# Attention scores from split operands, with the residual kept in DRAM and attention-stage weights in one buffer

## Chip, cores and metric

One NeuronCore of a Trainium2 chip runs the whole program. The time is the device time of one execution in microseconds (us); a comparison takes the median over executions.

## What is computed

The reference is a block with differential attention, a gated convolution and a gated feed-forward part, followed by two retention layers, all in float32, on 512 tokens of width 1024. The change touches the first block's attention:

```python
h = jnp.concatenate([meta, x], axis=1)           # 16 + 512 tokens
n = _rms(h, norm_mix_w[l])
z = n @ w_in[l]
q, k, v, glu, g_att, g_conv = jnp.split(z, splits, axis=-1)
...
s = jnp.einsum('bqhmd,bkhmd->bhmqk', qb, kf)     # 8 heads, two halves m of 64 each
mask = cid[None, :] <= qc[:, None]
p = jax.nn.softmax(jnp.where(mask, s, NEG_INF), axis=-1)
a = p[:, :, 0] - lam * p[:, :, 1]
return jnp.einsum('bhqk,bkhe->bqhe', a, vf)
...
h = h + m @ w_out[l]
```

## The kernel before

Activations lie transposed, features in partitions and tokens in columns. H (`o_h`) is the residual, K, Q and V_ the keys, queries and values of the 8 heads in float32, each head's two halves in rows 0 to 63 and 64 to 127. The large matrix products are made of three rounded (float32r) products: high weight by high input, high by low, low by high. For this, each weight slot of 128x1024 is split: ScalarE copies it into the rounded format (`high`, L1386), VectorE subtracts that from the raw weights (`low`, L2337). Raw weights come as units of 1 MB (256 columns by 8 k tiles, two slots each) from SyncE's queue (L3563) into three raw buffers of 8 KB per partition, unit u into buffer u % 3; a buffer is refilled once the last slot in it has been split. Units 28 to 31 are `w_conv_out`, 32 to 35 `w_out`, from 36 (`first_ffn`) on the feed-forward weights come through two buffers, and `S1T` and two more weight tiles lie where the third was.

All engines run fixed programs in order; semaphores (T, V, A, G for TensorE, VectorE, ScalarE, GpSimd) tie them, and an engine that waits holds back everything behind. The order around the change is written out by hand:

- 16 gate tiles (L870), each 48 products on TensorE, with the layer norm of the convolution beside them on VectorE and ScalarE: squares after gates 8 and 9, five diagonals (L2592) and a scaling after gate 12, for which TensorE waits when gate 12 is done.
- 32 attention steps i = 4h + r, head h, r = 0 to 3, whose query tile t comes from ORDER = (1, 2, 0, 3); t has 144 + 128 t key columns (t = 3: 16 and 512). TensorE does `scores(i)` (L888, plain float32), `turn(i-2)` (transposes of the probabilities, L899, L901), `values(i-3)` (L911, L913) and filler products of `conv_out_quarter` (L659: none at r=0, one quarter at r=1 and 2, two at r=3). VectorE does `combine(i-1)` (L2627 to L2635) and `highest(i)` (mask L2617, negated maximum L2621; the order of the two differs by r), then the convolution gating (L2664), at r=0 a weight split and the sum of a head (L2655), at r=1 the head's low part (`head_split`, L2659). ScalarE does `turn(i-2)` (L1622, L1625), `values(i-3)` (L1632, L1634) and `soften(i)` (exponentials with sums, L1614), at r=2 scalings of a finished head (L1640), at r=3 a weight split.
- Scores of t=0, 1, 2 use banks 0 and 1 or 2 and 3 in turn; t=3 needs all four, so it waits for the exponentials of both steps ahead of it.
- Then `w_out` (units 32 to 35) and `ffn_token` (L2776), which adds its result to H.

## Time and profile before

| | us |
|---|---|
| median of 3 runs | 1810.76 (1806.86 to 1813.85) |
| the profiled execution | 1809.18, span 1807.4 |
| TensorE busy | 1788.2 |
| VectorE busy | 1406.6 |
| ScalarE busy | 968.6 |
| mean granted TensorE clock | 0.999 of 2.4 GHz |

The page gives, for the slowest core, each engine's busy time, the span in slices, the chain of work that ended last and the costliest groups of instructions. The attention stage runs from about 354 to 484 us of the span, the gate stage before it from about 259.

### The profile page before, as it was taken

To read this page: it belongs to the slowest core of one execution; us is meant where nothing else is said; L and a number is where in the kernel's file an instruction comes from. 1 tells how busy PE (TensorE), PEld (TensorE's weight loads), DVE (VectorE), ACT (ScalarE), POOL (GpSimd) and SP (SyncE) were. 2 spreads that over 40 slices of the span, in tenths; PEclk is the share of its full clock that TensorE was granted. 3 is DMA by queue.
4 is the path that set the end of the run, shared out by engine and by line. 5 is a ranking of instruction groups with operands and counts; after the bars stand their busy time and mean duration, and the time that the engine had idled before them with its cause. 6 is when DMAs were issued, how large, how long until landed. Compare 5 with 4: busy or idle time off the path is not lost.

```text
span 1807.4 us, 32723 instructions
## 1 busy us (share of the span) xinstructions
PE 1788.2 (99%) x13606; PEld 1706.0 (94%) x13606; DVE 1406.6 (78%) x2464; ACT 968.6 (54%) x1894; POOL 164.5 (9%) x138
## 2 busy tenths in 40 slices
PE   9999999999999999999999999999999999999998
PEld 8999999978899989899899999999899999999987
DVE  5888897678756789869889797979358888888844
ACT  6223332568734447547566565657347566666632
POOL 0000000000000012011011212120000112121000
PEclk9999999999999999999999999999999999999999
DMA  5222222200132257566357777775333677777431
GB/s 198 94 81 84 94 94 71 94 24 25 63 108 74 79 136 169 128 158 146 107 125 156 158 157 153 158 154 126 117 94 81 131 163 149 160 150 162 116 118 70
DMA packets 251778, 213.47 MB, mean 118 GB/s; under 512 B 6646, under 2 KB 248111, under 8 KB 251630
## 3 DMA queue, kind: packets, MB, share of 16 engines
q1 hardware_dynamic: 185086, 178.34, 32.0%
q0 software_dynamic: 66528, 33.04, 14.9%
q8 instruction: 107, 1.75, 0.4%
q14 instruction: 41, 0.34, 0.1%
q10 hardware_dynamic: 16, 0.00, 0.0%
HBM read 209.26 MB, written 2.10 MB: 117 GB/s over the span
## 4 chain that ended last, share of the span: by engine, by line
PE 90%; DVE 5%; ACT 3%; DMA 1%; issue 0%; SPq 0%; DVEq 0%
PE ps L659 41%; PE ps L700 31%; PE ps L1300 5%; PE ps L1352 5%; DVE wlo L2337 1%; PE ps L888 1%; DMA raw<-in_w_up_dram 1%; PE ps L1141 1%; PE ps L1119 1%; PE ps L913 1%; PE ps L1132 1%; PE ps L1144 1%; ACT p L1614 1%; ACT whi L1386 0%; DVE ast L2621 0%
## 5 line engine op out<-in xcount | busy, mean ns | idle before, releaser
L2337 DVE TENSOR_TENSOR wlo<-raw,whi 128x1024 fp32r<-128x1024 f32 (+1 forms) x363 | 440.0, 1216 | 193.7 <-ACT whi L1386 192.3
L1386 ACT ACTIVATE whi<-raw 128x1024 fp32r<-128x1024 f32 (+1 forms) x363 | 380.6, 1050 | 245.3 <-PE ps L659 105.5
L659 PE MATMUL ps<-nhi,whi 128*128 128x256 f32 (+3 forms) x1392 | 316.8, 291 | 2.6 <-DVE clo L2605 0.8
L659 PE MATMUL ps<-nhi,wlo 128*128 128x256 f32 (+3 forms) x1392 | 312.5, 288 | 0.0
L659 PE MATMUL ps<-nlo,whi 128*128 128x256 f32 (+2 forms) x1264 | 275.4, 288 | 0.0
L659 PEld LDWEIGHTS ps<-nhi,whi 128*128 128x128 f32 x1392 | 227.3, 190 | 6.6 <-DVE clo L2605 1.0
L659 PEld LDWEIGHTS ps<-nhi,wlo 128*128 128x128 f32 x1392 | 226.4, 189 | 2.1
L700 PE MATMUL ps<-thi,whi 128*128 128x256 f32 x784 | 225.3, 287 | 1.2 <-DVE wlo L2337 0.5
L700 PE MATMUL ps<-thi,wlo 128*128 128x256 f32 x784 | 222.1, 283 | 0.0
L700 PE MATMUL ps<-tlo,whi 128*128 128x256 f32 x784 | 221.9, 283 | 0.0
L700 PE MATMUL ps<-nhi,whi 128*128 128x256 f32 (+1 forms) x756 | 216.1, 286 | 0.0
L700 PE MATMUL ps<-nhi,wlo 128*128 128x256 f32 (+1 forms) x756 | 213.3, 282 | 0.0
L700 PE MATMUL ps<-nlo,whi 128*128 128x256 f32 (+1 forms) x756 | 213.1, 282 | 0.0
L659 PEld LDWEIGHTS ps<-nlo,whi 128*128 128x128 f32 x1264 | 201.9, 189 | 1.9
L2507 DVE SCALAR_TENSOR_TENSOR c<-u,cv,c 128x514 f32<-128x514 f32 x240 | 163.2, 750 | 0.0
L700 PEld LDWEIGHTS ps<-thi,whi 128*128 128x128 f32 x784 | 150.0, 191 | 3.4 <-ACT kr L1410 1.4
L700 PEld LDWEIGHTS ps<-tlo,whi 128*128 128x128 f32 x784 | 150.0, 191 | 0.0
L700 PEld LDWEIGHTS ps<-thi,wlo 128*128 128x128 f32 x784 | 149.8, 191 | 0.0
L700 PEld LDWEIGHTS ps<-nhi,wlo 128*128 128x128 f32 x756 | 143.5, 190 | 0.0
L700 PEld LDWEIGHTS ps<-nlo,whi 128*128 128x128 f32 x756 | 143.3, 190 | 0.1
L700 PEld LDWEIGHTS ps<-nhi,whi 128*128 128x128 f32 x756 | 143.3, 189 | 0.1
L3504 POOL DMA_DIRECT2D raw<-in_w_in_dram x49 | 62.9, 1284 | 514.1 <-DMA raw<-in_w_in_dram 514.1
(473 smaller groups left out, 3655.8 us busy)
## 6 DMA issues: line engine op xcount, KB each, us to landing
raw<-in_w_in_dram SPq DMA_DIRECT2D x90, 1024.0 KB, 5.8
raw<-in_w_up_dram SPq DMA_DIRECT2D x22, 1024.0 KB, 5.2
raw<-in_w_out_dram SPq DMA_DIRECT2D x20, 1024.0 KB, 4.8
s1t<-in_w_in_dram SPq DMA_DIRECT2D x49, 256.0 KB, 3.1
s1t<-in_w_in_dram POOLq DMA_DIRECT2D x49, 256.0 KB, 7.1
raw<-in_w_in_dram POOLq DMA_DIRECT2D x49, 256.0 KB, 4.7
raw<-in_w_down_dram SPq DMA_DIRECT2D x16, 512.0 KB, 3.4
raw<-in_w_conv_out_dram SPq DMA_DIRECT2D x4, 1024.0 KB, 4.8
```

The source lines that it names most:

```text
L659: mm = eng.matmul(o, w, m[:, k, a:b], start=begins, stop=final and n == len(ks) - 1 and i == 2)
L700: mm = eng.matmul(o, w[:, k, :], m[:, k, :], start=start and k + i == 0, stop=stop and k == 3 and i == 2, skip_group_check=True)
L888: eng.matmul(sv[:, m, c0 + a:c0 + b], Q[r, h, 2 + 128 * t:130 + 128 * t], K[r, h, a:b], start=True, stop=True) \
L913: mm = eng.matmul(o, at_[:, j, :], V_[:, 1 + j, vc], start=False, stop=j == t)
L1119: mm = eng.matmul(P[:, z1 + 128 * n:z1 + 128 * n + 128], KR[c][:, x], QR[c][:, x], start=True, stop=True)
L1132: mm = eng.matmul(P[:, z + 128 * n:z + 128 * n + 128], KTK[:, n, :], VTK[:, n, 128 * c:128 * c + 128], start=True, stop=True)
L1300: mm = eng.matmul(P[:, 512 * b:512 * b + 256], x_[:, k, 128 * t:128 * t + 128], w_[:, k % 4, :], start=k + i == 0, stop=k == 7 and i == 2)
L1352: mm = eng.matmul(P[:, 512 * b:512 * b + 512], x_[:, k, 128 * t:128 * t + 128], w_[:, 0, w], start=k == 0 and i == 0, stop=k == 15 and i == 2)
L1386: eng.activation(hi, raw, ACT.Copy).then_inc(*A.up("hi", s))
L2337: eng.tensor_tensor(lo, raw, hi.bitcast(F), ALU.subtract).then_inc(*V.up("lo", s))
L2507: eng.scalar_tensor_tensor(C[:, f, :], src, c, C[:, f, :], ALU.mult, ALU.add).then_inc(*V.up("tap", f, tap))
L3504: eng.dma_start(quarters_of(v)[1], plan[v][0][:, 0:4, 0:128], accum_op=ALU.add).then_inc(*THIRD_IN[s1_of(v)].up("unit", v))
```

## The change

Four things together.

1. Keys and queries are split like weights: KHI, QHI are rounded copies by ScalarE (`key_high`, `query_high`), KLO, QLO the rest by VectorE (`key_low`, `query_low`), written over K and Q. A score is the sum of three rounded products (high by high, low query by high key, high query by low key) in one bank, for both halves.
2. KHI lies where H was. So H is written to a DRAM tensor `kept` early (at slot 8 of SyncE's queue, after the tokens are turned), and read back in four quarters after the last scores; each pair of `ffn_token` waits for its quarter.
3. QHI takes raw buffers 1 and 2. Units 29 to 32 therefore come one after the other through buffer 0; unit 33 (buffer 1) is loaded only after the last scores, and from there on two buffers alternate.
4. Keys are split at gates 10 to 13, the meta tokens and query 0 at gate 13, queries 1 and 2 at gate 14, and queries 3 to 7 at r=1 of heads 0 to 4.

```diff
--- before.py
+++ after.py
@@ -204,6 +204,10 @@
         V_ = at("v", [128, 5, D], F, o_v)
         Q = at("q", [128, NH, TQ], F, o_q)
         GA = at("ga", [128, NH, TQ], F, o_ga)
+
+        KHI, KLO = at("khi", [128, NH, T1], R, o_h), at("klo", [128, NH, T1], R, o_k)
+        QHI, QLO = at("qhi", [128, NH, T2], R, o_raw + 8192), at("qlo", [128, NH, TQ], R, o_q)
+        kept = nc.dram_tensor("kept", [128, KT, T1], F).ap()
 
         XT = at("xt", [128, 4, D], F, o_k)
         XM = at("xm", [128, D], F, o_k + 16384)
@@ -375,7 +379,9 @@
         assert len(place) == len(slots)
         before = [max((r for r in range(s) if place[r] == place[s]), default=None) for s in range(len(slots))]
         pairs_from = next(u for u in range(first_ffn, first_ffn + 3) if u % 3 == 0)
-        rawbuf = [u % 3 if u < pairs_from else (u - pairs_from) % 2 for u in range(len(plan))]
+        attention_from = first_ffn - 8
+        rawbuf = [u % 3 if u <= attention_from else 0 if u < first_ffn - 3 else (u - first_ffn) % 2 for u in range(len(plan))]
+        after_scores = first_ffn - 3
         follows = [next((v for v in range(u + 1, len(plan)) if rawbuf[v] == rawbuf[u]), None) for u in range(len(plan))]
         sevens = [u for u in range(len(plan)) if plan[u][1] is SEVEN]
 
@@ -592,11 +598,17 @@
         ROWS_IN, FM_IN, FR_IN, LAM_IN, CST_IN, POS_IN, FAR_IN, PBC_IN = [
             Signal(sem(f"{n}_in"), 16) for n in ("rows", "norm", "ffn_rows", "lambda", "const", "positions", "decay", "post")]
         EARLY_IN = [Signal(sem(f"early_in{i}"), 16) for i in range(2)]
+        H_OUT, H_IN = Signal(sem("h_out"), 16), [Signal(sem(f"h_in{i}"), 16) for i in range(4)]
         RAW_IN = [Signal(sem(f"raw_in{i}"), 16) for i in range(3)]
         QUARTER_IN, SUM_IN, THIRD_IN = [[Signal(sem(f"{n}_in{i}"), 16) for i in range(2)] for n in ("quarter", "sum", "third")]
         OUT_SENT = [Signal(sem(f"out_sent{i}"), 16) for i in range(5)]
-        signals = [T, V, A, G, *X_IN, ROWS_IN, FM_IN, FR_IN, LAM_IN, CST_IN, POS_IN, FAR_IN, PBC_IN, *EARLY_IN, *RAW_IN,
+        signals = [T, V, A, G, *X_IN, ROWS_IN, FM_IN, FR_IN, LAM_IN, CST_IN, POS_IN, FAR_IN, PBC_IN, *EARLY_IN, H_OUT, *H_IN, *RAW_IN,
                    *QUARTER_IN, *SUM_IN, *THIRD_IN, *OUT_SENT]
+
+        KEYS_AT = {10: (0, 1), 11: (2, 3, 4), 12: (5,), 13: (6, 7)}
+
+        def last_slot_of(u):
+            return max(s for s, slot in enumerate(slots) if slot[0] == u)
 
         def raw_in(u, k0=0):
             if u < 2 and k0 == 0:
@@ -881,12 +893,16 @@
             def scores(i):
                 h, t, nk = head(i)
                 sv, c0, banks = where(i)
+                qh, ql = QHI[:, (h + 4) % NH, 128 * t:128 * t + 128], QLO[:, h, 2 + 128 * t:130 + 128 * t]
                 for a, b in [(0, nk)] if t < 3 else [(0, NM), (NM, nk)]:
-                    for m in range(2):
-                        r = slice(64 * m, 64 * m + 64)
-                        on.wait_ge(A("q", h), A("k", h), *free(*banks[m]))
-                        eng.matmul(sv[:, m, c0 + a:c0 + b], Q[r, h, 2 + 128 * t:130 + 128 * t], K[r, h, a:b], start=True, stop=True) \
-                            .then_inc(*T.up("scores", i, m, a))
+                    kh, kl = KHI[:, h, a:b], KLO[:, h, a:b]
+                    for n, (q_, k_) in enumerate(((qh, kh), (ql, kh), (qh, kl))):
+                        for m in range(2):
+                            r = slice(64 * m, 64 * m + 64)
+                            on.wait_ge(A("qh", h), V("ql", h), A("kh", h), V("kl", h), A("kh_meta"), V("kl_meta"), *free(*banks[m]))
+                            mm = eng.matmul(sv[:, m, c0 + a:c0 + b], q_[r], k_[r], start=n == 0, stop=n == 2)
+                            if n == 2:
+                                mm.then_inc(*T.up("scores", i, m, a))
                 for m in range(2):
                     emptied(banks[m], A("exp", i, m))
 
@@ -1567,6 +1583,18 @@
                 on.wait_ge(V("centre", f), f > 1 and V("squares", f - 2))
                 eng.activation(SQ[f % 2], C[:, f, :], ACT.Square).then_inc(*A.up("ln_square", f))
 
+            def key_high(h):
+                on.wait_ge(A("k", h), H_OUT("sent"))
+                eng.activation(KHI[:, h, NM:T1], K[:, h, NM:T1], ACT.Copy).then_inc(*A.up("kh", h))
+
+            def key_high_meta():
+                on.wait_ge(A("k", 7), T("mini_scores"))
+                eng.activation(KHI[:, :, 0:NM], K[:, :, 0:NM], ACT.Copy).then_inc(*A.up("kh_meta"))
+
+            def query_high(h):
+                on.wait_ge(A("q", h), V("lo", last_slot_of(attention_from if h > 3 else attention_from - 2)))
+                eng.activation(QHI[:, (h + 4) % NH, :], Q[:, h, 2:TQ], ACT.Copy).then_inc(*A.up("qh", h))
+
             for i, (kind, f) in enumerate(GATES):
                 w.take()
                 w.done()
@@ -1593,6 +1621,12 @@
                 elif i == 13:
                     on.wait_ge(T("mini_scores"))
                     eng.activation(STS, P[0:NM, MB:MB + 32], ACT.Copy).then_inc(*A.up("mini_scores"))
+                    key_high_meta()
+                    query_high(0)
+                for h in KEYS_AT.get(i, ()):
+                    key_high(h)
+                for h in (1, 2) if i == 14 else ():
+                    query_high(h)
 
 
             def ln_split(fs):
@@ -1690,6 +1724,8 @@
                     head_scale(h - 2)
                 if r == 0 and h >= 3:
                     head_sum(h - 3)
+                if r == 1 and h < 5:
+                    query_high(h + 3)
 
 
             turn(30)
@@ -2570,6 +2606,18 @@
                 eng.tensor_scalar(nx[0:2, 4:5], P[0:2, 3076:3077], 1.0 / D, LN_EPS, ALU.mult, ALU.add).then_inc(*V.up("var_rest"))
                 rsqrt(("ln_rms",), rcol[:, 0:5], nx[:, 0:5], na[:, 0:5], V("var_rest"))
 
+            def key_low(h):
+                on.wait_ge(A("kh", h))
+                eng.tensor_tensor(KLO[:, h, NM:T1], K[:, h, NM:T1], KHI[:, h, NM:T1].bitcast(F), ALU.subtract).then_inc(*V.up("kl", h))
+
+            def key_low_meta():
+                on.wait_ge(A("kh_meta"))
+                eng.tensor_tensor(KLO[:, :, 0:NM], K[:, :, 0:NM], KHI[:, :, 0:NM].bitcast(F), ALU.subtract).then_inc(*V.up("kl_meta"))
+
+            def query_low(h):
+                on.wait_ge(A("qh", h))
+                eng.tensor_tensor(QLO[:, h, 2:TQ], Q[:, h, 2:TQ], QHI[:, (h + 4) % NH, :].bitcast(F), ALU.subtract).then_inc(*V.up("ql", h))
+
             for i in range(16):
                 w.take()
                 if i == 11:
@@ -2595,6 +2643,13 @@
                         on.wait_ge(A("ln_spread"), V("centre", f))
                         eng.scalar_tensor_tensor(C[:, f, :], C[:, f, :], cv[:, f, CLNW:CLNW + 1], LNR, ALU.mult, ALU.mult) \
                             .then_inc(*V.up("ln_scaled", f))
+                elif i == 13:
+                    key_low_meta()
+                    query_low(0)
+                for h in KEYS_AT.get(i, ()):
+                    key_low(h)
+                for h in (1, 2) if i == 14 else ():
+                    query_low(h)
 
 
             def ln_split(fs):
@@ -2735,6 +2790,8 @@
                     head_sum(h - 3)
                 if r == 1 and h >= 3:
                     head_split(h - 3)
+                if r == 1 and h < 5:
+                    query_low(h + 3)
 
 
             combine(31)
@@ -2772,7 +2829,7 @@
 
             def ffn_token(f):
                 j, c = f // 2, f % 2
-                on.wait_ge(*([T("out", 0, c, n) for n in range(2)] if j == 0 else [T("out", j, c)]))
+                on.wait_ge(H_IN[j]("in"), *([T("out", 0, c, n) for n in range(2)] if j == 0 else [T("out", j, c)]))
                 eng.tensor_tensor(H[:, f, Q0:T1], H[:, f, Q0:T1], tile_dst(PAIR["out", j, c], TQ)[0], ALU.add).then_inc(*V.up("out", f))
                 on.wait_ge(A("nh", f, False))
                 eng.scalar_tensor_tensor(NLO[:, f, 0:TQ], H[:, f, Q0:T1], cv[:, f, WFFN:WFFN + 1], NHI[:, f, 0:TQ].bitcast(F),
@@ -3493,7 +3550,7 @@
                     eng.dma_start(S1T[n % 2], plan[u][0][:, 4:8, 128:256], accum_op=ALU.add).then_inc(*SUM_IN[n % 2].up("unit", u))
 
             for s, (u, box, final) in enumerate(slots):
-                if rawbuf[u] == 2 and final and follows[u] is None:
+                if u == first_ffn - 1 and final:
                     first_sum(0)
                     first_sum(1)
                 if box_of(s)[1] == 1:
@@ -3538,7 +3595,7 @@
                     u = sevens[n]
                     if n > 1:
                         on.wait_ge(V("second_sum", sevens[n - 2]), V("lo", slot_of[sevens[n - 2], 1]))
-                    on.wait_ge(V("lo", raw2_read))
+                    on.wait_ge(V("lo", raw2_read), T("scored", 7))
                     eng.dma_start(S1T[n % 2], plan[u][0][:, 0:4, 128:256]).then_inc(*QUARTER_IN[n % 2].up("unit", u))
 
             raw2_read = max(s for s, (u, _, _) in enumerate(slots) if rawbuf[u] == 2)
@@ -3552,15 +3609,23 @@
                 elif s == len(slots) - 14:
                     on.wait_ge(T("mixed_all"))
                     eng.dma_start(PBC, post_norm_2[1:2, :].to_broadcast([128, D])).then_inc(*PBC_IN.up("in"))
-                if rawbuf[u] == 2 and final and follows[u] is None:
+                if u == first_ffn - 1 and final:
                     first_sum(0)
                     first_sum(1)
                 if box_of(s)[1] == 1:
                     first_sum(sevens.index(u) + 2)
+                if s == 8:
+                    on.wait_ge(A("h", 6, 1))
+                    eng.dma_start(kept, H).then_inc(*H_OUT.up("sent"))
                 v = follows[u]
-                if final and v:
+                if final and v and v != after_scores:
                     on.wait_ge(V("lo", s))
                     eng.dma_start(raw_of(v), plan[v][0]).then_inc(*RAW_IN[rawbuf[v]].up("unit", v))
+                if final and v == after_scores - 1:
+                    on.wait_ge(T("scored", 7), H_OUT("sent"))
+                    eng.dma_start(raw_of(after_scores), plan[after_scores][0]).then_inc(*RAW_IN[rawbuf[after_scores]].up("unit", after_scores))
+                    for j in range(4):
+                        eng.dma_start(H[:, 2 * j:2 * j + 2, :], kept[:, 2 * j:2 * j + 2, :]).then_inc(*H_IN[j].up("in"))
             for t in range(4):
                 for n, (f0, f1) in enumerate([(0, 8)] if t < 3 else [(0, 4), (4, 8)]):
                     on.wait_ge(V("out_ready", t, n))
```

ScalarE at r=1 and r=2 of head 2, before (i=9 and 10; `p` is the probabilities, `at` their transpose, `ps` PSUM):

```order
L1614 ACTIVATE p_1_114,ast<-ps,ast 128x400 [waits vector_done]
L1614 ACTIVATE p_1_117,ast<-ps,ast 128x400
L1622 ACTIVATE at_118<-ps 128x256 [waits tensor_done]
L1625 ACTIVATE at_118<-ps 16x128
L1614 ACTIVATE p_2_115,ast<-ps,ast 128x144 [waits vector_done]
L1614 ACTIVATE p_0_116,ast<-ps,ast 128x144
L1632 ACTIVATE os_123<-ps,ast 128x128 [waits tensor_done]
L1634 ACTIVATE ps,ss<-ps,ast 128x128 [waits scalar_done]
```

and in the change:

```order
L1648 ACTIVATE p_0_117,ast<-ps,ast 128x400 [waits vector_done]
L1648 ACTIVATE p_1_121,ast<-ps,ast 128x400
L1596 ACTIVATE qhi<-q 128x512
L1656 ACTIVATE at_122<-ps 128x256 [waits tensor_done]
L1659 ACTIVATE at_122<-ps 16x128
L1648 ACTIVATE p_1_118,ast<-ps,ast 128x144 [waits vector_done]
L1648 ACTIVATE p_0_120,ast<-ps,ast 128x144
L1666 ACTIVATE rbc<-ps,ast 128x128 [waits tensor_done]
L1668 ACTIVATE ps,ss<-ps,ast 128x128 [waits scalar_done]
```

The copy of a query stands behind both exponentials of t=2 (400 columns) and ahead of the transposes and the exponentials of t=0 (144 columns).

VectorE over the same steps, before, from the combination of t=1:

```order
L2635 SCALAR_TENSOR_TENSOR p_2_115<-p_0_116,ast,p_2_115 128x272 [waits vector_done]
L2617 MEMSET ps 64x2x64 [waits tensor_done]
L2372 SCALAR_TENSOR_TENSOR rcol<-na,rcol 128x4 [waits vector_done]
L2621 TENSOR_REDUCE ast<-ps 128x2 [waits vector_done]
L2617 MEMSET ps 64x2x64 [waits tensor_done]
L2364 SCALAR_TENSOR_TENSOR na<-rcol 128x4 [waits vector_done]
L2621 TENSOR_REDUCE ast<-ps 128x2 [waits vector_done]
```

and in the change:

```order
L2690 SCALAR_TENSOR_TENSOR p_2_119<-p_0_120,ast,p_2_119 128x272 [waits vector_done]
L2672 MEMSET ps 64x2x64 [waits tensor_done]
L2408 SCALAR_TENSOR_TENSOR rcol<-na,rcol 128x4 [waits vector_done]
L2676 TENSOR_REDUCE ast<-ps 128x2 [waits vector_done]
L2619 TENSOR_TENSOR qlo<-q,qhi 128x512 [waits scalar_done]
L2672 MEMSET ps 64x2x64 [waits tensor_done]
L2400 SCALAR_TENSOR_TENSOR na<-rcol 128x4 [waits vector_done]
L2676 TENSOR_REDUCE ast<-ps 128x2 [waits vector_done]
```

The subtraction, which waits for ScalarE's copy, stands between the maximum of t=2 (the first TENSOR_REDUCE) and the mask and maximum of t=0 (the second).

SyncE's queue from the second unit of `w_conv_out` to the last of `w_out`, before (raw_49, 50 and 51 are the raw buffers 0, 1 and 2):

```order
L3563 DMA raw_51<-in_w_conv_out_dram 128x8x256 [waits vector_done]
L3563 DMA raw_49<-in_w_conv_out_dram 128x8x256 [waits vector_done]
L3563 DMA raw_50<-in_w_conv_out_dram 128x8x256 [waits vector_done]
L3563 DMA raw_51<-in_w_out_dram 128x8x256 [waits vector_done]
L3563 DMA raw_49<-in_w_out_dram 128x8x256 [waits vector_done]
L3563 DMA raw_50<-in_w_out_dram 128x8x256 [waits vector_done]
L3563 DMA raw_51<-in_w_out_dram 128x8x256 [waits vector_done]
```

and in the change:

```order
L3623 DMA raw_49<-in_w_conv_out_dram 128x8x256 [waits vector_done] x3
L3623 DMA raw_49<-in_w_out_dram 128x8x256 [waits vector_done]
L3626 DMA raw_50<-in_w_out_dram 128x8x256 [waits h_out,tensor_done]
L3628 DMA h<-kept 128x1056 x4
L3623 DMA raw_49<-in_w_out_dram 128x8x256 [waits vector_done]
L3623 DMA raw_50<-in_w_out_dram 128x8x256 [waits vector_done]
L3623 DMA raw_49<-in_w_up_dram 128x8x256 [waits vector_done]
```

Three units in a row share buffer 0, and the second unit of w_out waits for TensorE, with the four reads of H behind it.

## Rows read from the trace of the kernel before

**Rows 1.** The page, busy time and share of TensorE (PE).
```profile
PE 1788.2 (99%) x13606; PEld 1706.0 (94%) x13606; DVE 1406.6 (78%) x2464; ACT 968.6 (54%) x1894; POOL 164.5 (9%) x138
```

**Rows 2.** Busy per stretch: us, PE, PEld, DVE, ACT, POOL, clock, DMA, GB/s.
```profile
366.92:384.70 17.78, 16.78 (x118) 13.57 (x118) 10.31 (x31) 10.65 (x38) 0.00 (x0) 0.90 0.00 1
...
413.31:427.96 14.65, 14.60 (x115) 12.13 (x115) 11.95 (x39) 12.19 (x43) 0.00 (x0) 1.00 0.22 73
```

**Rows 3.** The chain in order of time, attention: start, us, what.
```profile
398.73 1.28 PE ps L888 x8
...
424.53 0.98 DVE ast L2621
425.53 1.26 ACT p L1614 x4
...
427.19 0.72 ACT p L1614 x4
427.96 1.35 PE ps L888 x8
```

**Rows 4.** Timeline of TensorE, one head: start, us, line, operation.
```profile
433.72 0.73 PE L888 MATMUL ps<-k,q 64*128 64x272 f32 x4
434.38 0.28 PE L899 MATMUL ps<-ident,p 128*16 128x128 f32 x1
...
439.00 0.52 PE L888 MATMUL ps<-k,q 64*128 64x144 f32 x4
439.51 0.27 PE L899 MATMUL ps<-ident,p 128*16 128x128 f32 x1
```

**Rows 5.** Timeline: first records of 272 columns, loads; then means by form.
```profile
433.72 0.50 PE L888 MATMUL ps<-k,q 64*128 64x272 f32 x2
...
427.96 0.53 PEld L888 LDWEIGHTS ps<-k,q 64*128 64x128 f32 x8 [0.26 <-ACT p L1614]
...
L888 PE MATMUL ps<-k,q 64*128 64x400 f32 x24 | 5.7, 548 | 0.0
L888 PE MATMUL ps<-k,q 64*128 64x272 f32 x24 | 4.4, 442 | 0.0
```

**Rows 6.** The chain over the span: rounded products, 264 and 512 columns.
```profile
41.86 129.22 PE ps L659 x1056
...
1718.39 82.65 PE ps L1352 x363
```

**Rows 7.** Timeline: copies on ScalarE, subtractions on VectorE.
```profile
354.53 3.75 ACT L1602 ACTIVATE nhi<-c 128x514 fp32r<-128x514 f32 x7
...
357.95 2.50 DVE L2605 TENSOR_TENSOR clo<-c,nhi 128x514 fp32r<-128x514 f32 x4
```

**Rows 8.** Timeline of VectorE: mask and maximum of t=0.
```profile
440.76 0.17 DVE L2617 MEMSET ps<- 64x128 f32 x1
...
440.96 0.46 DVE L2621 TENSOR_REDUCE ast<-ps 128x2 f32<-128x288 f32 x1
```

**Rows 9.** Timeline of ScalarE: first exponential of t=2, heads 0 to 3.
```profile
364.07 0.59 ACT L1614 ACTIVATE p<-ps,ast 128x400 f32<-128x400 f32 x1 [1.71 <-DVE ast L2621]
...
380.42 0.59 ACT L1614 ACTIVATE p<-ps,ast 128x400 f32<-128x400 f32 x1
...
395.97 0.59 ACT L1614 ACTIVATE p<-ps,ast 128x400 f32<-128x400 f32 x1 [0.88 <-DVE ast L2621]
...
410.88 0.59 ACT L1614 ACTIVATE p<-ps,ast 128x400 f32<-128x400 f32 x1
```

**Rows 10.** Timeline: diagonals on VectorE, gate 12 on ScalarE.
```profile
331.51 0.99 DVE L2592 TENSOR_SCALAR sq<-ident,rcol 128x128 f32<-128x128 f32 x5
...
334.59 0.60 ACT L1580 ACTIVATE ga<-ps 128x514 f32<-128x514 f32 x1 [4.26 <-PE ps L659]
```

**Rows 11.** DMA issues of the page; then ScalarE's first split of unit 33.
```profile
raw<-in_w_conv_out_dram SPq DMA_DIRECT2D x4, 1024.0 KB, 4.8
...
485.10 1.04 ACT L1386 ACTIVATE whi<-raw 128x1024 fp32r<-128x1024 f32 x1
```

## Prediction

> **What bounds the kernel now.** I read the page first: TensorE is busy for 99% of the span [rows 1], so a thing costs time if it lengthens TensorE's own work or makes TensorE wait. The change lives in the attention stage, so next I cut the stretch view at the start of each head's last score step (query tile 3, "t=3"; within a head the order is t=1, 2, 0, 3). A settled head takes 14.65 us, with TensorE almost full but VectorE and ScalarE at 11.9 and 12.2 us [rows 2]: all three are near their limit, so the chain of waits must tell who leads. It does [rows 3]: up to 425.5 it runs on VectorE, which comes late to the 0.98 us maximum of t=2, then on ScalarE (exponentials of t=2, 1.26; of t=0, 0.72), and only then does TensorE start t=3 at 427.96. Head 2's t=3 at 398.73 follows in the same chain straight on TensorE's own products. So in heads 1 and 2 TensorE leads; from head 3 on, the loop is t=3's scores and the products after it, VectorE up to the maximum of t=2, ScalarE up to the exponential of t=0.
>
> **Scores on TensorE.** A float32 score product of 272 columns is two passes over two weight loads; the two halves of the head (rows 0 to 63, 64 to 127) run side by side. From its start to the next operation: 434.38 - 433.72 = 0.66 us for 272 columns, 0.51 for 144 (439.51 - 439.00) [rows 4]. The first two records last 0.50, the mean of all is 442 ns, so the second two last 0.39: the first pays about 0.11 us for a weight load in the open, the second's load is hidden behind the first's columns [rows 4, 5]. Loads of one pair after another come 0.113 us apart ((0.53 - 0.19) / 3) [rows 5]. Rounded (float32r) products take one pass: 129.22 / 1056 = 0.122 us for 264 columns, 82.65 / 363 = 0.228 for 512 [rows 6], 0.42 ns a column, against 0.83 x 2 for float32 ((548 - 442) / 128 per half). So four passes become three. A group costs 0.11 (first load) + 3 x the larger of 0.113 and the columns + 0.1 (the gap behind): 272 columns 0.11 + 0.35 + 0.1 = 0.56, saved 0.10; 400 columns 0.11 + 0.51 + 0.1 = 0.72 against 0.88 by the same law, saved 0.16; 144 columns 0.11 + 0.34 + 0.1 = 0.55 against 0.51, nothing saved, since loads set the pace; t=3 (16 + 512 columns) 0.45 + 0.64 + 0.1 = 1.2 against 1.28 (its 1.35 in [rows 3] less the 0.07 by which 0.73 exceeds 0.66), saved 0.1. No row has a rounded product under 256 columns or on 64 rows. Bounds: columns of the 144 form at the float32 price (0.24 a product) give 0.93, that is +0.4 a head; the two halves one after the other give rival B.
> Here a rule of the Trainium skill speaks against the change. The records say that a second load into the same rows was hidden [rows 4, 5]. The page TensorE: Matmul & The Clock Gate, section Part 3: Packing small matmuls, says that "LDWEIGHTS overlaps with in-flight MATMULs only when row_grp differs". By that rule each product would show its load; the trace of this kernel contradicts it, so I keep it as rival C.
> Where TensorE leads (heads 1, 2) 0.35 us a head is saved; in head 3 some 0.25; from head 4 only t=3's 0.1, since VectorE sets when t=2's maximum starts. Sum: -0.7 - 0.25 - 0.4 = **-1.35 us**.
>
> **The new splits inside the attention loop.** Heads 0 to 4 get `query_high` on ScalarE and `query_low` on VectorE at step r=1, for the head three further on. A copy of 514 columns takes ScalarE 0.62 (seven in 3.75: 0.52 apart), a subtraction takes VectorE 0.69 (four in 2.50: 0.60 apart) [rows 7]. The lengths matter less than the place. `query_low` waits for `query_high`, which is queued behind both exponentials of t=2; and behind `query_low`, on VectorE, wait the mask and maximum of t=0 (0.20 + 0.46 [rows 8]), which today run while ScalarE works on t=2. Behind these wait the exponential of t=0, and TensorE's t=3, whose banks it frees. From the start of t=2's exponential: 1.15 (both) + 0.62 + 0.05 + 0.60 + 0.20 + 0.46 + 0.1 + 0.72 + 0.05 = 3.95 us. I compare with today's distances [rows 2, 3, 9] (the starts of t=3 are the bounds of the stretches): head 4, 427.96 - 425.53 = 2.43, so +1.5; head 3, 413.31 - 410.88 = 2.43, +1.5; head 2, 398.73 - 395.97 = 2.76, +1.2; head 1, 384.70 - 380.42 = 4.28, nothing; head 0, 366.92 - 364.07 = 2.85 with a small copy of the 16-token part in it (0.2), +1.3. Sum **+5.5 us**. Bounds: below, 0.53 a head if VectorE came by chance to the subtraction with nothing due (+1.5 in all); above, the same 3.95 with head 1 uncovered, +6.5. I take 5.5, since the order on both engines is fixed.
>
> **Splits in the gate stage.** Eight keys, three queries and the meta tokens: about 11 x 0.53 = 5.8 us on ScalarE and 11 x 0.60 = 6.6 on VectorE between gates 10 and 14. They lie beside 30 us of TensorE work. The tightest place is gate 11: three keys put the weight split and the five diagonals back from 331.51 by some 1.6 us, so they would end at 331.51 + 0.99 + 1.6 = 334.1, and TensorE asks for them when gate 12 ends, about 334.5 [rows 10]. Cost 0; if that cover is short by some tenths, +0.3.
>
> **Transfers.** Keeping H is one write of 2.16 MB at slot 8 and four reads after the last scores. A 1 MB unit lands in 4.8 us [rows 11]; by size the write takes some 10 us in a stage in which a buffer is refilled two units ahead. With one buffer, the next convolution unit starts after the split of the last one and is wanted three steps later, some 10 us; it needs 4.8. Unit 33 now starts only after t=3 of head 7 (about 473) and lands near 478; its first split runs at 485.10 [rows 11], 7 us spare. H arrives in quarters until about 486; the additions that want it follow TensorE's first w_out tiles, whose last weights are split after 485.10. Cost 0; what would be late next is unit 33, and each us past 485 would be one us of TensorE.
>
> **Sum.** The profiled execution took 1809.2 us (span 1807.4); -1.35 + 5.5 = +4.1, so **1813 us**. That execution lies 1.6 under the median of the runs, well inside their spread. A measurement of this kernel tells about 0.5%, 9 us, from no change; this is within it.
>
> **Rivals.**
> A, the forecast: a new wait of ScalarE and VectorE eats more than the passes give. 1813. Chance 0.60.
> B, the one that ends slower: rounded products on 64 rows do not run side by side. For: no row shows such a pair. Against: float32 halves start together. A group then has six products in a row: t=3 2.2 instead of 1.28, t=2 1.27, t=1 0.92, t=0 0.86. It decides as soon as the pair's second half waits for the first; heads 1 and 2 lose 1.6 each, heads 3 to 7 about 1.1 to 1.25: +9 in place of -1.35, 1809.2 + 5.5 + 9 = 1824. Chance 0.09.
> C, each product shows its weight load (the rule above), or a narrow operand is no quicker: 0.21 more a group, twice in t=3, is +4; the narrow form alone is +0.4 in four heads, 1.6. 1815 to 1817. Chance 0.10.
> D, the clock. In head 0's long period the granted clock is 0.90 of 17.78 us, which is 1.8 / 0.5 = 3.5 us at 1.2 instead of 2.4 GHz; TensorE was busy in it for 16.78 only [rows 2]. That cost some 1.7 us. Four heads now get a wait of 1.2 to 1.5 us. If each brings such a fall, +1.7 to +6.8: 1815 to 1820. Against: the stretch up to head 4's t=3 holds 1.00 though it too ends in a wait [rows 2, 3]. The Trainium skill, same page, section A second HAM failure mode: psum-queue depth-cycling, says that short idle times between groups of matmuls make the clock swing between its levels; by that rule this case is the likely one, and in the trace only one of the eight heads bears it out. Chance 0.12.
> E, the new chain is mostly covered and only the passes count: 1808 to 1810. For: ScalarE and VectorE each have over 2 us free a head. Chance 0.07.
> F, the change does more than it says, over 9 us gained: even all passes saved without any wait give 8 x 0.35 = 2.8. Chance 0.02.
>
> **Numbers.** Slower by over 0.5% means beyond 1818: B whole, the upper half of D, and 0.02 for a late unit or H: 0.17. Faster 0.02. Within 0.5%: 0.81. The range takes A with its bounds (1809 to 1815), C, E and most of D: 1806 to 1820.
>
> **What would show it.** Right: score groups of 0.56 and 0.72 us with both halves starting together; on VectorE, in heads 2 to 4, a wait of the subtraction for the query's copy of about 0.6 to 1 us and TensorE idle 1.2 to 1.5 us before t=3; heads 5 to 7 at about 14.5 us; no wait for unit 33 or H. Wrong: halves one after another, more than one stretch at 1.2 GHz, a wait of the first w_out split for its load, or heads 2 to 4 still at 14.6.

## The result, and the profile after

The changed kernel takes 1816.84 us (median of 4 runs, 1815.78 to 1819.14) against 1808.81 for the kernel before on the same chip (4 runs, 1806.56 to 1813.85): a ratio of 1.0051, 95% interval 1.0035 to 1.0066. On a second chip it took 1818.98 (4 runs) against 1806.48 (14 runs), 1.0061, 1.0040 to 1.0082. The forecast was 1813, with a range of 1806 to 1820. So the time lies in the range and about 4 us above the forecast. Both intervals lie clear of 1: the change makes the kernel slower, by half a per cent. In the forecast's own terms the ratio stands just beyond the 0.5% inside which it put the result with a chance of 0.81, though the intervals reach to both sides of that mark. The profiled execution took 1817.56, with a span of 1815.8, 8.4 more than before.

TensorE's share on the page after, for [rows 1]. It is busy for 1.6 us more, in a span that is 8.4 us longer:

```profile
PE 1789.8 (99%) x13686; PEld 1713.8 (94%) x13686; DVE 1416.4 (78%) x2481; ACT 978.6 (54%) x1911; POOL 164.6 (9%) x138
```

Busy time per stretch after, as [rows 2], each from one start of t=3 to the next (us, PE, PEld, DVE, ACT, POOL, clock, DMA share, GB/s). The first ends with t=3 of head 1, the last with that of head 6:

```profile
368.41:386.07 17.66, 16.53 (x126) 14.23 (x126) 10.02 (x26) 10.80 (x37) 0.00 (x0) 0.90 0.00 1
386.07:402.52 16.45, 14.16 (x121) 12.45 (x120) 12.97 (x51) 10.98 (x39) 0.00 (x0) 1.00 0.20 65
402.52:420.37 17.85, 15.95 (x126) 14.10 (x126) 12.54 (x41) 12.87 (x44) 0.00 (x0) 0.90 0.00 1
420.37:436.63 16.26, 14.35 (x124) 12.81 (x124) 12.44 (x41) 12.85 (x44) 0.00 (x0) 1.00 0.21 65
436.63:452.80 16.17, 15.95 (x124) 14.10 (x125) 12.03 (x40) 12.21 (x43) 0.00 (x0) 0.89 0.01 2
452.80:467.40 14.60, 14.38 (x124) 12.84 (x124) 11.94 (x39) 12.20 (x43) 0.00 (x0) 1.00 0.22 74
```

Before, the first of these was 17.78 at a clock of 0.90 [rows 2]; the stretch of head 2, cut in the same way, was 14.03, and those of heads 3 to 6 were 14.64 to 14.67. Two different things make the new lengths. Stretches two and four are long at full clock: TensorE stands idle for some 2 us of each. Stretch five has no new split in front of its end and is almost as busy as it is long, but its clock is 0.89. Stretch three has both. So the table already says: a new wait, and more time at 1.2 GHz.

The chain after, for [rows 3], first the way into t=3 of head 4, then the long pieces on which the later stages can be lined up:

```profile
432.53 1.26 ACT p L1648 x4
433.79 0.53 ACT qhi L1596
...
434.35 0.69 DVE qlo L2619
435.05 0.17 DVE ps L2672
...
435.28 0.44 DVE ast L2676
435.75 0.84 ACT p L1648 x4
...
436.63 1.74 PE ps L903 x12
...
501.71 47.41 PE ps L671 x396
...
719.85 9.33 DMA raw<-in_w_up_dram
729.46 6.62 DMA raw<-in_w_up_dram
...
1726.79 82.62 PE ps L1368 x363
```

This is the path of the prediction, item by item: both exponentials of t=2, the copy, the subtraction, mask, maximum, exponentials of t=0, t=3. From 432.53 to 436.63 it is 4.10 us, where 3.95 was forecast and 2.43 stood before. The first long row, the start of the stage with `w_out`, came at 491.66 before and comes at 501.71: the attention cost 10.05 us. Of these, 0.23 stood already when the first long stretch of products began, and the rest can be seen from here (before, then after):

```profile
216.45 90.08 PE ps L659 x744
```

```profile
216.68 90.08 PE ps L671 x744
```

From there to the start of `w_out` it was 491.66 - 216.45 = 275.21 us and is 501.71 - 216.68 = 285.03, 9.82 more. The last row came at 1718.39 [rows 6] and comes at 1726.79: only 8.40 of the 10.05 arrive. In this pair of executions the difference sits at the two transfers that the chain waits for: 9.84 and 7.70 us before, 9.33 and 6.62 after. It is not a return for coming late. From the start of `w_out` to the last row the kernel before took 1226.73 us and this execution of the change 1225.08; a second one, late as well, took 1227.88, and the kernel with the transfers of the change alone, which is not late, 1223.60. This part differs by up to 4.5 us between executions, whatever comes ahead of it.

Waits after (engine, line, for whom: us in all, times, longest), and TensorE's wait before a t=3:

```profile
DVE qlo L2619 <- ACT qhi L1596: 6.8, 5, 1.9
PEld ps L903 <- ACT p L1648: 6.5, 6, 1.9
```

```profile
402.52 0.28 PE L903 MATMUL ps<-khi,qhi 64*128 64x16 f32 x2 [1.64 <-ACT p L1648]
...
389.24 0.39 PE L671 MATMUL ps<-nhi,whi 128*128 128x256 f32 x1 [0.66 <-DVE m L2719]
```

The second row is a wait that the prediction did not have. It comes from head 1, on VectorE:

```profile
383.63 0.69 DVE L2619 TENSOR_TENSOR qlo<-q,qhi 128x512 fp32r<-128x512 f32 x1 [1.85 <-ACT qhi L1596]
...
385.91 0.16 DVE L2740 TENSOR_SCALAR ones_d<-ps 128x16 f32<-128x16 f32 x1
...
388.62 0.23 DVE L2745 SCALAR_TENSOR_TENSOR ga<-ones_d,wsub,ga 128x16 f32<-128x16 f32 x1
388.77 0.42 DVE L2719 TENSOR_TENSOR m<-ps,m 128x258 f32<-128x258 f32 x1
```

Between the subtraction and the gating (`m`, L2719) stand fourteen operations on 16 columns, 0.2 us apart. They begin as late as the row of work ahead of them lets them, none waits for another engine, and the gating behind them frees its bank late; TensorE's filler products wait for it.

### The profile page after: what moved, and what is told of

It reads as the page before. It is cut to its first block, busy times and chain, and to the rows that moved or that the text cites. A ratio compares the mean times of both kernels' runs of the same rounds, so it can differ in the third digit from the quotient of the medians.

```text
span 1815.8 us, 32929 instructions
## 1 busy us (share of the span) xinstructions
PE 1789.8 (99%) x13686; PEld 1713.8 (94%) x13686; DVE 1416.4 (78%) x2481; ACT 978.6 (54%) x1911; POOL 164.6 (9%) x138
## 4 chain that ended last, share of the span: by engine, by line
PE 87%; DVE 7%; ACT 4%; DMA 1%; issue 0%; SPq 0%; DVEq 0%
PE ps L671 40%; PE ps L712 31%; PE ps L1316 5%; PE ps L1368 5%; DVE wlo L2373 2%; ACT p L1648 1%; DMA raw<-in_w_up_dram 1%; DVE ast L2676 1%; PE ps L1157 1%; PE ps L1135 1%; PE ps L903 1%; PE ps L1160 1%; PE ps L1148 1%; DVE p L2690 0%; ACT whi L1402 0%
```

## The experiments

Seven kernels ran, in two groups, each group on one chip: the change once more, head 1's splits alone and one product instead of three on one, the others on another. Times are compared across the groups by their ratios to the kernel before, which ran in both (1806.48 and 1806.85 us). "Period of head k" is the time from the start of t=3 of head k-1 to that of head k. Without a fall of the clock the changed kernel has 16.1, 16.45, 16.26, 16.26 for heads 1 to 4 and 14.6 behind; the kernel before has (17.7 with a fall), 14.03, 14.64, 14.65, 14.65.

**The change once more.** No edit.

> The changed kernel itself once more, beside its variants. If the stretches at 1.2 GHz come from the waits before t=3, they are again at heads 2 and 4 or others of heads 1 to 4 (a period above 16.3 us where one falls, 16.2 without), and the time is 1814 to 1818 us, 8 over the kernel before. If they are chance of one execution, this one shows none in the attention and 1813 us.

1818.98 us, 12.5 above the kernel before, where I expected 8. Of its periods for heads 2 to 5 (16.45, 16.27, 16.26, 16.16) the second and the last:

```profile
402.95:419.22 16.27, 14.39 (x124) 12.84 (x124) 12.44 (x41) 12.84 (x44) 0.00 (x0) 1.00 0.01 2
...
435.48:451.64 16.16, 15.95 (x124) 14.13 (x124) 12.02 (x40) 12.19 (x43) 0.00 (x0) 0.89 0.01 2
```

TensorE's waits before t=3 repeat to a hundredth (1.63, 1.72 and 1.73 us; 1.64, 1.72 and 1.73 in the first execution). The fall in head 3's period is gone, that in head 5's is there again. So the path is fixed and the falls are not: which waits bring one differs between executions. Over the eight executions of the change the mean granted clock was 0.994 to 0.997; over the fourteen of the kernel before on this chip 0.997 to 1.000. The means of these are 0.9955 and 0.9984. A clock lower by 0.003 is 0.003 x 1807 = 5.4 us of lost full speed, wherever in the span it falls, so by this estimate falls carry a large part of the 8.0 and 12.5 us.

**The subtraction later.** `query_low` behind the maximum of t=0 (r=2); the copy stays.

```diff
-                if r == 1 and h < 5:
-                    query_low(h + 3)
...
+                if r == 2 and h < 5:
+                    query_low(h + 3)
                 if r != 2:
                     highest(i)
```

> The changed kernel with one call moved: query_low of heads 3 to 7 stands on VectorE behind the mask and maximum of t=0 instead of ahead of them; query_high stays. Theory (the place on VectorE costs, through the wait for ScalarE's copy): the way from the exponential of t=2 to t=3's scores loses the 0.05 + 0.60 of the subtraction and the 0.66 of mask and maximum, which run beside ScalarE again, and keeps ScalarE's copy of 0.53. Of 1.4 to 1.7 us of idle time before t=3 in heads 0, 2, 3 and 4 some 0.5 is left; the late token chain of head 1 is gone. That is 4 x 1.1 + 1, some 5 us, and if the two further falls of the clock came of those waits, 3 more: 5 to 8 us under the changed kernel, 1809 to 1812. Rival (the subtraction's own 0.6 us on a full VectorE costs, wherever it stands): under 1 us gained, 1816.

1808.02 us (11 runs), ratio 1.0002, 0.9993 to 1.0011. The chain into t=3 of head 4:

```profile
426.29 1.26 ACT p L1648 x4
427.55 0.52 ACT qhi L1596
...
428.48 0.72 ACT p L1648 x4
...
429.25 0.83 PE ps L903 x7
```

VectorE has left this path; the copy alone stretches the 2.43 us of before to 429.25 - 426.29 = 2.96. Periods of heads 2 to 4 are 14.88, 15.12 and 15.13. TensorE's waits before t=3 are 0.50 to 0.59, and no period of the attention ran below full clock. The same work in the same numbers, one subtraction a few places later, is worth 9 to 11 us (0.0049 and 0.0059 in the ratio). I had expected 1809 to 1812, with the falls gone; so the direction and the cause were as expected and the gain somewhat larger.

**Both later.** The copy at the end of r=3, the subtraction behind the maximum of t=3 of the next head.

```diff
+                if r == 3 and h < 5:
+                    query_high(h + 3)
...
+                if r == 3 and 1 <= h < 6:
+                    query_low(h + 2)
```

> The changed kernel with query_high at the end of r=3, behind the weight split, and query_low at r=3 of the head after, behind the maximum of t=3, where VectorE waits for the filler products. Theory: nothing waits for either; TensorE idle before t=3 as before the change (under 0.3 us in heads 3 and 4), one stretch at 1.2 GHz, and only the shorter products are left: 1.35 us under the kernel before, 1807 to 1808. If the splits were dear by their length, 0.5 to 1 us a head stays: 1811 to 1813. If the transfers or the gate stage cost something, it stays too, and shows here as a time over the kernel before with heads at 14.5 us.

1805.21 us (11 runs), ratio 0.9994, 0.9986 to 1.0003: the lowest median of all kernels here, and not to be told from the kernel before. Two of its periods, and its chain at the start of `w_out`:

```profile
384.66:398.59 13.93, 13.93 (x122) 12.41 (x121) 12.21 (x45) 10.12 (x36) 0.00 (x0) 1.00 0.24 77
413.22:427.82 14.60, 14.38 (x124) 12.83 (x124) 12.53 (x40) 12.73 (x44) 0.00 (x0) 1.00 0.21 73
```

```profile
491.35 47.41 PE ps L671 x396
```

ScalarE and VectorE still do the five copies and five subtractions (12.73 and 12.53 busy in a period, 12.19 and 11.95 before), at no cost: 14.60 against 14.65. The stage with `w_out` starts at 491.35 against 491.66, and the stretch ahead began at 216.59 against 216.45: 274.76 against 275.21. These 0.45 us are all that the cheaper scores give; 1.35 was forecast.

**Transfers alone.** The scores as before, in float32 from K and Q, no splits; H in DRAM, one buffer, unit 33 and the reads of H after the last scores as in the change.

```diff
-                    for n, (q_, k_) in enumerate(((qh, kh), (ql, kh), (qh, kl))):
...
+                        eng.matmul(sv[:, m, c0 + a:c0 + b], Q[r, h, 2 + 128 * t:130 + 128 * t], K[r, h, a:b], start=True, stop=True) \
```

> The changed kernel without any split of keys and queries and with the float32 scores of before; H still goes to DRAM and comes back, units 29 to 32 still go through buffer 0, unit 33 still waits for the last scores. Theory (transfers are hidden): the time of the kernel before within 1 us, heads at 14.65, the first split of unit 33 not waiting. Rival (a late unit or H): a wait of ScalarE for raw weights near 485 or of VectorE for H, 1 us or more each, and the time over 1810.

1806.75 us (11 runs), ratio 0.9998, 0.9989 to 1.0006. Periods of 14.64 to 14.67 from head 3 on. The DMA issues between 200 and 500 us (KB each, median us to landing) show that the reads are slow for their size and still hidden:

```profile
raw<-in_w_out_dram SPq DMA_DIRECT2D x4, 1024.0 KB, 4.9
h<-kept SPq DMA_DIRECT2D x4, 528.0 KB, 8.1
```

**TensorE kept busy in the wait.** Ahead of t=3 of heads 2, 3 and 4, seven float32 products of 128 columns into a free bank, whose result nobody reads.

```diff
+                if r == 3 and h in (2, 3, 4):
+                    b_fill = SPARE["head", h - 2]
+                    on.wait_ge(*free(b_fill))
+                    for _ in range(7):
+                        eng.matmul(P[:, 512 * b_fill:512 * b_fill + 128], ones, ones, start=True, stop=True)
```

> The changed kernel with seven float32 products of ones by ones (1.54 us by the 0.11 of a record) on TensorE ahead of t=3's scores of heads 2, 3 and 4, into the bank that the head's transposes overwrite later. They fill a wait of 1.6 to 1.7 us, so they cost nothing themselves. Theory D (idle time before t=3 brought the two further stretches at 1.2 GHz): one stretch is left instead of three, 3 to 3.4 us gained, 1813 to 1814. Rival (the falls come of something else, such as products on 64 rows): three stretches remain, the time within 1 us of the changed kernel.

1815.30 us (5 runs), ratio 1.0047, 1.0033 to 1.0061. The periods of heads 3 and 4:

```profile
403.20:419.46 16.26, 15.94 (x139) 14.41 (x140) 12.44 (x41) 12.85 (x44) 0.00 (x0) 1.00 0.01 2
419.46:435.74 16.28, 15.93 (x138) 14.40 (x139) 12.44 (x41) 12.84 (x44) 0.00 (x0) 1.00 0.19 65
```

The path is untouched (16.26), TensorE is busy across it (15.94 against 14.35), and no period runs below full clock; head 5, 16.17 in the change, is back at 14.58. From t=3 of head 0 to t=3 of head 7 it takes 108.87 us against 113.61 in the change; 1.55 of that is head 1's period (16.11 against 17.66), ahead of which no fill stands. That is one execution, and the falls vary. But the granted clock of the timed runs is on record too: 0.997 to 0.999 in the five executions of this kernel, mean 0.9976, against 0.994 to 0.997, mean 0.9955, in the eight of the change, and a mean of 0.9986 in the 27 of the kernel before beside it. So most of the lost clock is back. The times show less of it: a ratio of 1.0047 lies only 0.0004 to 0.0014 (0.7 to 2.5 us) below the change's two, with intervals that overlap. This profiled execution also gave some back at the very start: its long first stretch of products began at 44.34 where that of the change began at 42.09, with a granted clock of 0.50 from 10 to 15 us, where the change has 1.00. So the fill removes the falls where it is placed; what it is worth in time over many executions stays open. It gives nothing back of the wait itself: the period stays 16.26.

**Head 1's splits alone.** Only the two splits that head 1 issues go to the late places.

```diff
-                if r == 1 and h < 5:
+                if r == 1 and h < 5 and h != 1:
                     query_low(h + 3)
...
+                if r == 3 and h == 2:
+                    query_low(h + 2)
```

> Only the two splits that head 1 issues move to the places of low cost (the copy to the end of r=3, the subtraction to r=3 of head 2); heads 0, 2, 3 and 4 stay as in the change. Theory: the head 1 to 2 period goes from 16.45 back to 13.9 to 14.1, because VectorE's small operations on the 16 token part are no longer pushed, heads 2 to 4 keep 16.2 (or 17.8 with a fall of the clock), and the time falls by 1.5 to 2.4 us, to about 1814.5 to 1815.5. Rival (head 1 is late because head 0 was late): head 1 keeps 16 us and nothing is saved.

1816.61 us (5 runs), ratio 1.0055, 1.0034 to 1.0077. The period of head 2:

```profile
386.29:401.86 15.57, 13.97 (x122) 12.39 (x122) 12.11 (x46) 10.74 (x37) 0.00 (x0) 1.00 0.21 69
```

My expectation gave all of that period's excess to head 1 and was wrong: it fell from 16.45 to 15.57 and not to 14. The period also holds head 2's own splits at r=1, which this kernel keeps. So head 1's splits cost 0.88, through the wait of the filler products (the gating ran at 387.95 instead of 388.77, and TensorE's 0.66 us wait is gone), and head 2's own cost 15.57 - 14.03 = 1.54. The rival of the expectation (head 1 late because head 0 was) is out as well: head 0's first t=3 was as late here. This execution has falls in the periods of heads 3 and 4 (17.87 and 17.84, each at a clock of 0.90), and none in head 1's (16.11) or head 5's (14.58). The time, 1816.61, is 2.4 below the change beside it, at the large end of the gain that I expected (the time itself lies above the 1814.5 to 1815.5 expected); but the intervals overlap, so the 0.88 rests on the period alone.

**Where the clock fell.** The rows of all nine profiled executions together: before t=3 of heads 2, 3 and 4 TensorE waited 1.60 to 1.74 us in the three executions of the change and of "head 1's splits alone", nine waits, and five of the periods behind them hold a fall. In the six other executions the same waits are at most 0.6 us or filled, eighteen places, and none of these periods holds one. Head 1's period is another matter: it holds a fall in five of the nine, among them the kernel before (a wait of 0.68 ahead of it) and "both later" (0.67), and none in two with a wait of 1.92 and one of 0.78. That fall is not of the change's making.

**One product instead of three.** As "both later", but with only high query by high key.

```diff
-                    for n, (q_, k_) in enumerate(((qh, kh), (ql, kh), (qh, kl))):
+                    for n, (q_, k_) in enumerate(((qh, kh),)):
```

> The splits in the places of low cost, and of the three products of each score only high query by high key: it leaves out low query by high key and high query by low key. Theory A (my step for TensorE: columns of scores count in full where TensorE leads): heads 1 and 2 get shorter by another 0.8 us each, heads 3 to 7 by what t=3 saves (0.4), in all 3 to 3.6 us under the 1805.2 of the version with three products, 1802. Rival (VectorE's chain of combinations and maxima sets the head, and TensorE's saving is lost in a wait behind it): heads 3 to 7 stay at 14.5 to 14.6, head 2 at 13.8 or more, in all less than 1 us.

1805.37 us (10 runs), ratio 0.9991, 0.9978 to 1.0004, where theory A said 1802: the rival's result. From head 3 on a period is 14.55 to 14.57, as the rival had it, against 14.60 to 14.63 in "both later". A head's period and the chain behind t=3:

```profile
426.34:440.90 14.56, 13.69 (x105) 11.65 (x106) 12.52 (x40) 12.57 (x44) 0.00 (x0) 1.00 0.01 2
```

```profile
426.34 0.61 PE ps L903 x4
...
427.48 1.10 PE ps L936 x4
```

In the version with three products the two rows are 1.30 and 0.44. The 0.69 saved at t=3 is lost a little later, where four transposes of a finished head (L936) now take 1.10. The timeline says for whom they wait:

```profile
426.93 1.27 ACT L1673 ACTIVATE os<-os,rcol 128x128 f32<-128x128 f32 x4
...
427.66 0.14 PEld L936 LDWEIGHTS ps<-ident,os 128*128 128x128 f32 x1 [0.15 <-ACT os L1673]
```

So for t=3's part my rival named the wrong engine: it is ScalarE's scalings, behind the exponentials of t=0, which run beside t=3 and set the pace once t=3 is short. What t=1, 2 and 0 save is hidden by VectorE, as the rival said: the same chain runs on VectorE from 432.12 to 438.44. TensorE is free for 0.87 us of such a period, and fewer products give the end 0.05 of it. Only where TensorE leads do they count: head 1's period is 16.60 against 17.60 (a fall in both) and head 2's 13.71 against 13.93.

## Why the prediction came out as it did

**The direction and the path were right.** The wait of the subtraction for the copy, and of everything behind it, is in the chain as forecast; TensorE's new idle time before t=3 is 1.64 to 1.73, forecast 1.2 to 1.5, and the subtraction waits 1.25 to 1.85 for the copy, forecast 0.6 to 1. The path came to 4.10 and not 3.95: the exponentials of t=0 show 0.84 of their length and not 0.72, the subtraction 0.69 and not 0.60, and the gap behind the maximum is shorter by 0.07.

**Split terms: "+5.5", measured about +7.1.** Head 0: t=3 starts at 368.41 instead of 366.92, +1.5 with 0.23 from the start of the program, so 1.26; forecast 1.3. Head 1, "nothing": nothing in its own period (17.66 against 17.7), but 0.88 in the next. That step of the working failed: I priced the subtraction by t=3 of the same head and did not follow the rest of VectorE's row of work, though the text says that what is queued behind counts. Head 2: 1.54, and 1.64 with the saving taken out; forecast 1.2. Heads 3 and 4: 16.26 - 14.64 = 1.62, and some 0.05 more with the saving; forecast 1.5.

**TensorE's saving: "-1.35", measured -0.45.** Groups from their start to the next operation, in head 2 where TensorE never stops (kernel before, then both later):

```profile
391.83 0.94 PE L888 MATMUL ps<-k,q 64*128 64x400 f32 x4
392.71 0.28 PE L899 MATMUL ps<-ident,p 128*16 128x128 f32 x1
...
395.23 0.52 PE L888 MATMUL ps<-k,q 64*128 64x144 f32 x4
395.68 0.28 PE L899 MATMUL ps<-ident,p 128*16 128x128 f32 x1
```

```profile
391.73 0.45 PE L903 MATMUL ps<-khi,qhi 64*128 64x400 f32 x2
392.02 0.34 PE L903 MATMUL ps<-khi,qlo 64*128 64x400 f32 x2
392.20 0.35 PE L903 MATMUL ps<-klo,qhi 64*128 64x400 f32 x2
392.47 0.28 PE L915 MATMUL ps<-ident,p 128*16 128x128 f32 x1
...
395.10 0.34 PE L903 MATMUL ps<-khi,qhi 64*128 64x144 f32 x2
...
395.59 0.28 PE L915 MATMUL ps<-ident,p 128*16 128x128 f32 x1
```

400 columns: 0.88 and 0.74 (forecast 0.88 and 0.72). 272 columns: 0.66 and 0.58 (0.56). t=3: 1.28 and 1.24 (1.2). 144 columns: 0.45 and 0.49 (0.55), a loss. The law of columns and loads was right to 0.06 a group; the groups give 0.22 a head where 0.35 was forecast, and the period only 0.10 (13.93 against 14.03). From head 3 on the product run shows why little of even t=3's part arrives. So this term was mis-sized in both places: 0.1 a head was let through from head 3 on where 0.05 or less came, and 0.35 in heads 1 and 2 where 0.1 came.

**Clock: rival D came on top.** It was given a chance of 0.12 as a case of its own; in the profiled executions it comes together with the forecast's path. "More than one stretch at 1.2 GHz" was among the signs of being wrong, and it is there. Two further stretches at 1.2 GHz cost 17.85 - 16.26 = 1.6 and 16.17 - 14.60 = 1.6. The granted clock around one, with TensorE idle for 4.13 - 2.40 = 1.7 us just ahead of it:

```profile
432.50:436.63 4.13, 2.40 (x21) 2.19 (x19) 2.87 (x11) 3.08 (x12) 0.00 (x0) 1.00 0.42 150
...
437.50:441.00 3.50, 3.50 (x21) 2.85 (x18) 2.76 (x8) 1.63 (x6) 0.00 (x0) 0.54 0.00 0
```

My argument against D was that the stretch up to head 4's t=3 ended in a wait at a clock of 1.00; but that wait was short: the first record carries 0.26 [rows 5], and the new ones are 1.6 to 1.7. For heads 2 to 4 the falls come with these waits and go when the wait is filled or shortened, though not every wait brings one (five of nine). The Trainium skill (TensorE: Matmul & The Clock Gate, A second HAM failure mode: psum-queue depth-cycling) says that frequent short idle times between groups of matmuls make the clock swing, and by it I had called D the likely case; the runs side with it in part, by the same five of nine.

**The sum again.** Path +7.1, saving -0.45, falls +3.2 make +9.85; from the long stretch at 216 us to the start of `w_out` it is +9.82. The program ends 8.4 later, since the part behind was 1.65 shorter in this execution, which is the scatter of that part and no effect of the change. In the medians it is +8.0 and +12.5, against a forecast of +4.1. So the path was right and three sizes were too favourable: the splits by 1.6, the saving by 0.9, and the falls, which the sum put at nothing, by 3.2. That the time still lies in the range is partly luck: the range was drawn wide enough for most of D.

**What cost nothing, cost nothing.** Gate stage: from the long stretch at 216 us to the last one of the stage it takes 342.46 - 216.68 = 125.78 us, and took 342.23 - 216.45 = 125.78. Transfers: no wait for unit 33 or H in the list, and 0.9998 when done alone. Rival B (halves apart) is out: pairs of 400 columns start 0.18 us apart (392.02, 392.20), which is the 0.42 ns a column of a single product [rows 6], so both halves run in that time. Rival C is out by the same pace, since each pair has its own loads into the same rows; its narrow part came to 0.04 a group of 144 columns. The rule of the Trainium skill (TensorE: Matmul & The Clock Gate, Part 3: Packing small matmuls), that such loads don't overlap, does not hold here.

## What to carry to other kernels

When work is put into a loop in which two engines hand to each other, its place can cost more than its length: the same copy and subtraction cost 10 to 12 us in one place (ratios of 1.0051 and 1.0061 against 0.9994) and nothing in another. Price an insertion by all that is queued behind it on its engine until the next idle time, into the next iteration too. And when an insertion makes TensorE wait 1.6 or 1.7 us in every head, as here, count some falls of its clock as part of the likely case: five of nine such waits had one, at 1.6 us each.

## What I had not expected of the hardware

- Waits of 1.64 to 1.73 us in front of a score group are followed in some executions by 3.5 us at a granted clock of 0.54, in others at the same place by none. Each costs 1.6 us. With TensorE kept busy across three of them, or the wait cut to 0.6, none came in the periods behind them. The fall in head 1's period comes and goes with a short wait too, in the kernel before as well.
- Three rounded products on 64 rows take 0.49 us at 144 columns, with pairs 0.11 us apart (395.28, 395.39 in "both later") where 144 columns at 0.42 ns would be 0.06, where plain float32 takes 0.45. Of the widths here the format gains from 272 columns on (0.58 against 0.66).
- Reads of 528 KB in 128 rows, four issued at once behind a 1 MB unit, land in 8.1 us, where 1 MB units land in 4.9 ("transfers alone"; 7.3 and 5.5 in the change).
- The part from the start of `w_out` to the last row takes 1223.60 to 1228.05 us in the nine profiled executions, with no relation to how late it starts: at the transfers of the feed-forward weights each execution waits differently.
